# Output projection as seven half-size products, with the gate folded into sums of its weights

## The reference

```
mod = silu(c) @ ada_w + ada_b;  shift, scale, gate = split(mod, 3)
h   = rms_norm(x, norm_w) * (1 + scale) + shift
p   = h @ w_in                      # twelve kinds of columns, 4624 in all
...                                 # two mixers give o_g and o_h
m   = g_a * (o_g @ w_up_gla) + g_b * (o_h @ w_up_hgrn)
x   = x + gate * (m @ w_out)
out = rms_norm(x, final_norm_w)
```

## Time and profile before

| | us |
|---|---|
| median of 3 runs | 2876.27 |
| the profiled execution's own time | 2875.79 |
| its span, first to last instruction | 2874.0 |
| TensorE busy | 2841.4 (99%) |
| VectorE busy | 1525.2 (53%) |
| ScalarE busy | 1274.9 (44%) |
| GpSimd busy | 166.4 (6%) |
| mean granted clock of TensorE, of full speed | 0.998 |

### The profile page before, as it was taken

One profiled execution on the slowest core, in us unless ns is written; L12 is line 12 of the kernel. 1 busy time (PEld: TensorE's weight loads), 2 busy tenths in 40 slices (PEclk: granted clock), 3 DMA queues, 4 the chain that ended last, 5 costly groups with the idle time before them and its releaser, 6 DMA issues.

```text
span 2874.0 us, 38189 instructions
## 1 busy us (share of the span) xinstructions
PE 2841.4 (99%) x14534; PEld 2333.7 (81%) x14534; DVE 1525.2 (53%) x2004; ACT 1274.9 (44%) x1683; POOL 166.4 (6%) x281
## 2 busy tenths in 40 slices
PE   6999999999999999999999999999999999999998
PEld 4888888788887888888888888888888888888887
DVE  6455455644556444564555635546355463645634
ACT  3643336433473334633446433464335633355332
POOL 1010000100001000010000100001000010000100
PEclk9999999999999999999999999999999999999999
DMA  8223442233422443324432243322433224342232
GB/s 322 95 82 119 132 147 89 82 132 129 138 89 81 132 133 133 96 74 138 141 124 92 74 150 128 127 90 73 155 124 128 92 75 156 110 135 88 80 125 73
DMA packets 90205, 336.40 MB, mean 117 GB/s; under 512 B 9936, under 2 KB 10192, under 8 KB 88464
## 3 DMA queue, kind: packets, MB, share of 16 engines
q1 hardware_dynamic: 89744, 333.45, 34.9%
q10 hardware_dynamic: 256, 0.20, 0.0%
HBM read 316.63 MB, written 16.78 MB: 116 GB/s over the span
## 4 chain that ended last, share of the span: by engine, by line
PE 98%; DMA 1%; DVE 0%; ACT 0%; SPq 0%; POOL 0%; issue 0%; POOLq 0%; DVEq 0%; ACTq 0%
PE A L1041 46%; PE F L1052 33%; PE A L1103 12%; PE R L1139 1%; PE F L1166 1%; PE A L1181 1%; PE F L1160 1%; DMA ada_w<-in_ada 1%; PE R L1132 1%; PE R L1166 0%; PE R L1206 0%; PE R L1205 0%; PE R L1181 0%; PE R L988 0%; PE A L999 0%; DVE ada_w L721 0%
## 5 line engine op out<-in xcount | busy, mean ns | idle before, releaser
L676 DVE TENSOR_TENSOR w_lo<-w_raw,w_hi 128x1024 fp32r<-128x1024 f32 (+1 forms) x480 | 588.6, 1226 | 1051.0 <-ACT w_hi L453 1048.6
L453 ACT ACTIVATE w_hi<-w_raw 128x1024 fp32r<-128x1024 f32 (+1 forms) x480 | 507.3, 1057 | 753.3 <-PE A L1041 480.6
L1041 PE MATMUL A<-w_hi,h_hi 128*128 128x512 f32 (+1 forms) x1536 | 582.6, 379 | 0.0
L1041 PE MATMUL A<-w_lo,h_hi 128*128 128x512 f32 (+1 forms) x1536 | 572.9, 373 | 0.0
L1041 PE MATMUL A<-w_hi,h_lo 128*128 128x512 f32 (+1 forms) x1536 | 572.6, 373 | 0.0
L1052 PE MATMUL F<-h_hi,w_hi 128*128 128x512 f32 x1408 | 553.8, 393 | 0.0
L1052 PE MATMUL F<-h_hi,w_lo 128*128 128x512 f32 x1408 | 548.2, 389 | 0.0
L1052 PE MATMUL F<-h_lo,w_hi 128*128 128x512 f32 x1408 | 548.2, 389 | 0.0
L1041 PEld LDWEIGHTS A<-w_hi,h_hi 128*128 128x128 f32 x1536 | 288.3, 188 | 60.8 <-issue 9.0
L1041 PEld LDWEIGHTS A<-w_hi,h_lo 128*128 128x128 f32 x1536 | 288.5, 188 | 51.7
L1041 PEld LDWEIGHTS A<-w_lo,h_hi 128*128 128x128 f32 x1536 | 288.7, 188 | 47.7 <-issue 0.2
(11 more groups left out here) (180 smaller groups left out, 2790.4 us busy)
## 6 DMA issues: line engine op xcount, KB each, us to landing
w_raw<-in_w_stream SPq DMA_DIRECT2D x464, 512.0 KB, 3.5
xy<-in_x SPq DMA_DIRECT2D x8, 2048.0 KB, 8.7
result<-xy SPq DMA_DIRECT2D x32, 512.0 KB, 3.5
xf<-in_xt SPq DMA_DIRECT2D x30, 512.0 KB, 4.2
xn<-in_x SPq DMA_DIRECT2D x28, 512.0 KB, 4.9
ada_w<-in_ada SPq DMA_DIRECT2D x12, 1024.0 KB, 20.0
w_raw<-in_w_stream SPq DMA_DIRECT2D x16, 544.0 KB, 6.0
xy<-in_x SPq DMA_DIRECT2D x4, 512.0 KB, 13.9
```

Source lines behind the costliest of these rows:

```text
L453: AF(w_hi[:, s % RING, 0:n], w_raw[:, s % RAW, 0:n], ACT.Copy).then_inc(w_hi_done.sem, 1)
L676: V.tensor_tensor(w_lo[:, s % RING, 0:n], w_raw[:, s % RAW, 0:n], w_hi[:, s % RING, 0:n].bitcast(fp32), ALU.subtract).then_inc(w_split.sem, 1)
L1041: last = mm(A[t][:, 0:width], src[ia][:, k, t * P:(t + 1) * P], w_[iw][:, s % RING, kk * width:(kk + 1) * width], start=(k == 0 and n == 0 ...
```

## The change

**Seven products.** m is cut in halves of the frames (256 each) and in two halves of the features, w_out in halves of its rows and columns. Instead of eight half-size products (192 matmuls per block) there are seven, on sums and differences of the halves. A half-size product is two slots with 12 matmuls each, so the output projection has 14 slots (52 to 65) and 168 matmuls. Feature tiles are dealt to the two halves in turn (FEAT), so that pairs of tiles can be added up as they come. The pairs of banks that receive the products are `OUT_BANK`; three products are added up on top of an earlier one that VectorE has already taken (`PRODUCTS`, last field False).

**Sums of weights.** The pieces of w_out, times the gate, and their sums are made once, by GpSimd in block 0 (`out_pieces`), and written to DRAM (`pieces`, 14 of 128 by 1024). All blocks read their weights of slots 52 to 65 from there.

**Sums of m.** In every block GpSimd makes four sums of each pair of tiles (`m_sums`, four operations of 128 by 256, each waiting for the one before), ScalarE rounds them (`s_high`), and GpSimd makes the low part of three pairs (`s_low`), VectorE that of the last.

**Output.** VectorE no longer multiplies by the gate. It adds the banks into `xy` in 16 additions (`ADDS`). `xy` shares its place with the sums of m, so it is loaded later, in four parts (slots 54 and 57 of SyncE). ScalarE squares in slots 62 and 65.

**Gate later.** Parts 4 and 5 of `ada_w` are loaded behind the weights of slots 0 to 3, and worked off during slots 1 to 7 of block 0.

**Other.** `w_raw` of slots 60 to 65 uses three of its four buffers. Two of the four steps of `x_scale` and `h_low` move to slot 65. F0 uses the banks A2, A3, F0, F1.

```diff
-SLOTS = OUT0 + 8
+SLOTS = OUT0 + 14
+FEAT = [0, 4, 1, 5, 2, 6, 3, 7]
+PRODUCTS = [("m", 0, 0, 0, True), ("m", 1, 0, 1, True), ("s", 1, 1, 2, True), ("s", 0, 0, 0, False),
+            ("s", 1, 0, 2, False), ("m", 1, 1, 1, True), ("s", 0, 1, 0, False)]
+ADDS = {3: [(0, 0, 0, 0, 0), (0, 1, 1, 0, 0), (1, 0, 0, 0, 1), (1, 1, 1, 0, 2)],
+        6: [(2, 0, 2, 1, 0), (2, 1, 3, 1, 0)],
+        7: [(0, 0, 0, 1, 0), (0, 1, 1, 1, 0)],
+        9: [(2, 0, 0, 1, 7), (2, 1, 1, 1, 8)],
+        11: [(1, 0, 2, 0, 0), (1, 1, 3, 0, 0)],
+        13: [(0, 0, 2, 0, 11), (0, 0, 2, 1, 5), (0, 1, 3, 0, 12), (0, 1, 3, 1, 6)]}
-XN_AT = [49, 51, 53, 56]
+X_SCALE_AT = [49, 50, 65, 65]
+H_LOW_AT = [50, 51, 65, 65]
+RAW_AT = [s % RAW if s < 60 else (s - 60) % 3 for s in range(SLOTS)]
...
 @block.sync
             load_w(0)
-            for n in (4, 5):
-                sp.wait_ge(ada_pe, n - 3)
-                load_ada(n)
-            load_row(gate_b[:, :], 1792 + 2 * D, gate_b_in)
             for j in (2, 3):
                 load_w(j - 1)
                 load_pair(0, j, first=True)
             load_w(3)
+            sp.wait_ge(x_sq.sem, x_sq.at(0, 4))
+            load_ada(4)
+            load_row(gate_bc[:, :], 1792 + 2 * D, gate_b_in)
...
+                    if first and s == 0:
+                        sp.wait_ge(ada_pe, 4)
+                        sp.wait_ge(modT, 4)
+                        load_ada(5)
...
+                    if s in (54, 57):
+                        for t in (0, 1) if s == 54 else (2, 3):
+                            if t < 3:
+                                sp.wait_ge(s_lo_pool.sem, s_lo_pool.at(b, t + 1))
+                            else:
+                                sp.wait_ge(s_lo_dve.sem, s_lo_dve.at(b, 1))
+                            sp.dma_start(xy[:, t, :], x[bass.ds(b * T + t * P, P), :]).then_inc(xy_in[t // 2].sem, 16)
...
 @block.gpsimd
+            def out_pieces():
...
+                def gated(i, q):
+                    pool.wait_ge(b_in[i], 16 * (q + 1))
+                    two = w_b[:, i, :].rearrange("p (k n) -> p k n", k=2)
+                    cols_ = slice(512 * (i % 2), 512 * (i % 2) + 512)
+                    done(G(two, two, gate_bc[:, cols_].unsqueeze(1).broadcast_to([P, 2, 512]), ALU.mult))
+                for q in range(2):
+                    if q == 0:
+                        pool.wait_ge(ada_pe, 5)
+                    else:
+                        pool.wait_ge(pieces_out, 16 * stored[0])
+                    for i, part in ((0, 0), (2, 2), (3, 6), (1, 4)):
+                        pool.dma_start(w_b[:, i, :], w_stream[OUT0 + part + q, :, 0:1024]).then_inc(b_in[i], 16)
+                    if q == 0:
+                        pool.wait_ge(mg_used.sem, 16)
+                    for i, piece in ((0, B11), (2, B21), (3, B22)):
+                        gated(i, q)
+                        store(i, piece + q)
+                    gated(1, q)
+                    pool.wait_ge(pieces_out, 16 * stored[0])
+                    done(G(w_b[:, 0, :], w_b[:, 1, :], w_b[:, 0, :], ALU.subtract))
+                    store(0, T1 + q)
...
+            def m_sums(b, jp):
+                early, late = slice(0, T // 2), slice(T // 2, T)
+                a, c = m_raw[:, 2 * jp, :], m_raw[:, 2 * jp + 1, :]
+                pool.wait_ge(m_split.sem, m_split.at(b, 2 * jp + 2))
+                G(c[:, late], a[:, late], c[:, late], ALU.add).then_inc(m_link.sem, 1)
+                pool.wait_ge(m_link.sem, m_link.at(b, 3 * jp + 1))
+                G(a[:, late], a[:, early], a[:, late], ALU.subtract).then_inc(m_link.sem, 1)
...
+            def s_low(b, jp):
+                pool.wait_ge(s_hi_done.sem, s_hi_done.at(b, jp + 1))
+                two = slice(2 * jp, 2 * jp + 2)
+                nc.gpsimd.tensor_tensor(s_lo[:, two, :], m_raw[:, two, :], s_hi[:, two, :].bitcast(fp32),
+                                        ALU.subtract).then_inc(s_lo_pool.sem, 1)
...
+                m_sums(b, 0)
+                m_sums(b, 1)
                 if not last:
                     for t in range(NT):
                         x_tile(b + 1, t)
+                m_sums(b, 2)
+                s_low(b, 0)
+                s_low(b, 1)
+                m_sums(b, 3)
+                s_low(b, 2)
...
 @block.scalar
+            def s_high(b, jp):
+                act.wait_ge(s_sum.sem, s_sum.at(b, jp + 1))
+                two = slice(2 * jp, 2 * jp + 2)
+                AF(s_hi[:, two, :]..., m_raw[:, two, :]..., ACT.Copy).then_inc(s_hi_done.sem, 1)
...
                     if not (last and s + RING >= SLOTS):
                         split_hi(b if s + RING < SLOTS else b + 1, (s + RING) % SLOTS)
                     if s in UP_SLOT:
                         j = UP_SLOT[s]
+                        if j == KT - 1:
+                            for jp in range(3):
+                                s_high(b, jp)
                         act.wait_ge(up_used.sem, up_used.at(b, j + 1))
...
+                    if s == OUT0:
+                        s_high(b, 3)
+                    if s == OUT0 + 10:
+                        for t in (0, 1):
+                            y_square(b, t)
...
+                    if s == SLOTS - 1:
+                        for t in (2, 3):
+                            y_square(b, t)
...
 @block.vector
-                            V.tensor_tensor(y_tmp, A[t][:, :], gate_bc[:, cols_], ALU.mult).then_inc(out_used.sem, 1)
-                            dve.wait_ge(out_used.sem, out_used.at(b, 4 * n + t + 1))
-                            ins = V.tensor_tensor(xy[:, t, cols_], xy[:, t, cols_], y_tmp, ALU.add)
...
+                    if first and s in (1, 3):
+                        gate_partial(s // 2)
+                    if first and s in (5, 7):
+                        gate_column(s // 7)
...
+                    if s == OUT0 + 2:
+                        dve.wait_ge(s_hi_done.sem, s_hi_done.at(b, 4))
+                        V.tensor_tensor(s_lo[:, 6:8, :], m_raw[:, 6:8, :], s_hi[:, 6:8, :].bitcast(fp32),
+                                        ALU.subtract).then_inc(s_lo_dve.sem, 1)
+                    if s - OUT0 in ADDS:
+                        i = s - OUT0
+                        if i in (3, 6):
+                            dve.wait_ge(xy_in[i // 6].sem, xy_in[i // 6].at(b, 32))
+                        for pair_, tt, t, half, behind in ADDS[i]:
+                            if behind:
+                                dve.wait_ge(y_add.sem, y_add.at(b, behind))
+                            tile = xy[:, t, half * 512:half * 512 + 512]
+                            V.tensor_tensor(tile, tile, OUT_BANK[pair_][tt][:, :], ALU.add).then_inc(y_add.sem, 1)
...
-                    if s == 59:
-                        for t in range(NT):
+                    if s in (OUT0 + 12, OUT0 + 13):
+                        for t in (0, 1) if s == OUT0 + 12 else (2, 3):
...
 @block.tensor
-            modulation(4)
-            modulation(5)
...
+                    n, q = divmod(s - OUT0, 2)
+                    kind, f, half, pair_, fresh = PRODUCTS[n]
...
+                    if n < 2:
+                        pe.wait_ge(m_split.sem, m_split.at(b, 4 * q + 3 + n))
+                    if n == 2:
+                        if q == 0:
+                            pe.wait_ge(mg_used.sem, mg_used.at(b, 16))
+                            pe.wait_ge(s_lo_pool.sem, s_lo_pool.at(b, 2))
+                        else:
+                            pe.wait_ge(s_lo_pool.sem, s_lo_pool.at(b, 3))
+                            pe.wait_ge(s_lo_dve.sem, s_lo_dve.at(b, 1))
+                    if q == 0 and n >= 3:
+                        pe.wait_ge(y_add.sem, y_add.at(b, (2, 6, 4, 8)[n - 3]))
...
+                    if first and s in (4, 6):
+                        modulation(4 + s // 6)
```

246 lines of the change are left out of this document (144 added, 102 removed).

## The result

The changed kernel took **2919.60 us** (median of 4 runs, 2918.11 to 2922.01) against 2876.25 us for the kernel before on the same chip: a ratio of 1.0152, 95% interval 1.0134 to 1.0170. It is 43 us slower. The forecast was 2888, slower by 11.7 us, in a range from 2834 to 2903: the direction was right and the size was not, and the time lies above the range.

A forecast was written before the change was run, and what follows sets the result against it. TensorE, busy 99% of the span, was taken as the bound. Once −4.8, per block 8 × (5.3 + 0.95 − 5.44) = +6.5, boundaries +3.5 and clock +6.5 gave +11.7 us: 2888 us, range 2834 to 2903.

The forecast's parts named there:

- The earlier start: Before block 0: slot 0 starts at 41.8 instead of 51.2 us, −9.3 us.
- What block 0 gives back: Block 0: low clock at the start +1, modulation steps moved between slots +2.0, GpSimd's weight pieces holding up VectorE +1.5.
- Slot 60: The fifth product waits for VectorE's additions 5 and 6 behind the split of 61: 0.95 us late every block.
- Rivals 1 and 2: Output projection: GpSimd not held up by VectorE, 2857 us, chance 0.23; GpSimd near its lower bound, 2839 us, chance 0.20.
- the new chain at slot 56: ScalarE's s_high(3) and the split of 56 wait behind GpSimd's chain: TensorE 5.3 us late at slot 56.
- Sharing with VectorE: Slots 52 to 55: GpSimd loses 3.1 us beside VectorE's operations with two SBUF inputs, bounds 0 and 3.1.
- VectorE: m_lo of j = 7 then ends at 5.1 ... That still serves slot 55: After slot 52 starts: m_lo ends at 5.1 us instead of 3.9, still in time for slot 55, due at 8.2.
- The list of 38 us: VectorE's work in the 14 output slots: splits, additions, s_lo, x_scale, h_low and norms, 38 us in 38.1.
- Rival 3: Every block falls to the low clock and GpSimd wins over VectorE's split, making slot 55 late: 2903 us, chance 0.12.
- the block's end: Turn to the next block: the split for its slot 3 stands behind VectorE's norms, 0.5 us late seven times, 3.5 us.
- the clock: After slot 56's wait TensorE falls to the low clock in half the blocks: 4 × 1.6 = 6.5 us, bounds 0 and 21.
- SyncE's waits ... Nothing: Slots 52 to 65: SyncE's waits for s_low hold back the load of 59, which still has 4 us; no cost.

The follow-up runs named there:

- Experiment 1: Changed kernel with GpSimd's low parts of the sums of m cut to 8 of 512 columns, matmuls reading the high part instead: 2899.81 us.
- experiment 7: The kernel with all sums of m and low parts on VectorE (2860.72 us), with only the sums of m given back to GpSimd: 2869.26 us.
- experiment 6: Changed kernel with all sums of m and low parts on VectorE, h_low of the second pair at slot 55, s_high later, last squares first: 2860.72 us.
- Experiments 8 to 12: Boundary edits to the changed kernel: squares earlier (2904.87 us), loop written out (2911.21), that with two result stores behind weight loads (2899.22), stores alone (2916.98), all three (2895.68).
- experiment 8: Changed kernel with ScalarE's last two squares of a block ahead of h_high of the next block's last two pairs: 2904.87 us.
- experiment 4: Changed kernel with the three low parts that GpSimd made moved to VectorE, GpSimd keeping only the sums: 2952.36 us.
- experiment 9: Changed kernel with the loop over blocks written out on all five engines: 2911.21 us.
- experiments 13 and 14: The kernel before with only the later gate loading, with its loop (2869.98 us) and with the loop written out (2869.17 us).

## Why the prediction was right or wrong

**Right.** The removed matmuls are 5.44 us a block. The earlier start is −9.7 us (forecast −9.3). What block 0 gives back is +4.7 (forecast 1 + 2.0 + 1.5 = 4.5), but that this agrees is partly luck: the low clock at the start cost 2.4, not 1, the modulation steps 1.7, and GpSimd's pieces 0.2, not 1.5; the last 0.4 is the row of roots at slot 48. GpSimd's operations take 2.39 and 0.74 us (forecast 2.3 and 0.7). Slot 60 is 1.14 us late by the distance of the matmuls (forecast 0.95). Rivals 1 and 2 fell: GpSimd is held (1.59 us for an addition of 0.74 beside VectorE), and its operations are not near the lower bound.

**Wrong in place, and right in length by luck: the new chain at slot 56.** In the last block it stands as forecast to 0.4 us. In the seven others two things were wrong. The step named "Sharing with VectorE" let only GpSimd lose time; "no row shows VectorE being held" was true of the trace before, and I took it for nothing instead of bounding it. Held, VectorE took 3.98 us for 1.41 us of h_low, and 3.41 for a split of 1.22. And the step "VectorE: m_lo of j = 7 then ends at 5.1 ... That still serves slot 55" left h_low of the next block's second pair out of VectorE's list between m_lo and the split of 55. The list of 38 us does not show it either: it has x_scale and h_low of two pairs, as many as slot 65 alone has. Together slot 55 is 4.6 us late, slot 56 0.6, slot 60 1.1: 6.3 us, against 5.3 + 0.95 = 6.25. That the two errors moved the wait by one slot and hardly changed its length is luck; the chain itself was later than forecast, with s_high(3) 14.1 us after slot 52 in block 1 instead of 12.9.

**Rival 3 came nearest.** It had slot 55 late because GpSimd wins over VectorE, and the low clock in every block, and both came. It had a chance of 0.12 and a time of 2903, still 17 us short, since it too left the block's end at 3.5 us and gave slot 55's wait no price of its own.

The Trainium skill (SBUF — State Buffer, SBUF: two separate sides) says that of a GpSimd operation and a VectorE operation with two inputs in SBUF, whichever starts first blocks the other for its whole instruction. The trace now agrees in both directions: 0.69 to 1.48 us for m_lo and 1.22 to 3.41 for a split on VectorE, 0.74 to 1.59 for an addition on GpSimd. Experiment 1 shows what it costs by leaving out the low parts with the order unchanged, experiment 7 by giving the sums back to GpSimd; experiment 6 changed the order too.

**Mis-sized: the clock.** "I take half the blocks: 4 × 1.6" gave 6.5 us. The size of one fall was right (1.6 us at slot 55), but it came in all eight output projections, 13 us, and behind slot 3's wait in three blocks, 4.9 us. By the mean granted clock, (1 − 0.990) × 2920 − (1 − 0.998) × 2874 = 23 us of TensorE's full-speed time was lost to it, though part of this fell into waits and cost nothing. Output projection in all: forecast 8 × (6.25 − 5.44) + 6.5 = 13.0, measured 25.5. Of the 12.5 between them 6.5 are the clock, 3.2 are slot 0 of the next block, 0.4 to 0.8 late in blocks 2 to 6, and the rest is spread over slots 55 to 61.

**The step that failed most: "The block's end ... 0.5 us late, seven times, 3.5. Bounds 0 and 1.5 each".** It measured 26.0 us in all, 3.7 each. Slot 3 is 2.2 to 2.7 us late in blocks 1 to 6 and 0.5 in the last, 15.3 in sum; from slot 3 to slot 4 6.9 are lost, 4.9 of them at the lower clock and the rest mostly in waits for slot 4's weights; the row of roots takes 3.2, and 0.6 is the rest. The 3.2 us of slot 0 come on top, in the output projections' sum. The table load I named and didn't add, and the standstill of 2.5 us ahead of it can't be seen before: there the idle of the earlier trace rows is ended by TensorE. Experiments 8 to 12 show the parts: without the loop 1.9 us of slot 3's wait goes, and with it slot 0's; the stores behind the loads take slot 4's wait; and the earlier squares alone take slot 3's wait as well, since ScalarE is then through sooner. "SyncE's waits ... Nothing" looked only at slot 59: at the block's end four stores that wait for the norms stand ahead of the loads for slots 4 and 5.

The profiled execution is 34.5 us over the sum (46.2 against 11.7): 22.5 are the boundary, 12.5 the output projection, and the start with block 0 and the rest are 0.2 and 0.3 the other way.

**Left open.** Why the standstill at the loop's head is 2.5 us on ScalarE in the changed kernel and 1.3 to 1.6 in experiment 8, which changes only the order of some instructions, and grew to 6 us on VectorE in experiment 4, with no edit there. The Trainium skill (Runtime: NRT & Kernel Launch, Instruction fetch mechanics) says that a taken branch whose target is outside the two pages held forces a fetch before execution goes on. This would fit: the length differs between kernels whose code differs, it goes when the loop goes, and it is missing ahead of the last block, where no engine jumps back. No run here varied the layout alone or measured the fetch, so this cause is not shown. The share of order and of sharing in slot 55's wait is open too, beyond what experiments 1 and 7 say.

## What to carry to other kernels

Work moved to GpSimd is not free when VectorE is busy in the same stretch (34.5 of 47 us here). Take its whole duration as the upper bound of what VectorE loses, and compare that with simply doing it on VectorE (1.2 us against 2.4 here); the sums of m, moved alone in experiment 7, cost a good 1 us a block. When matmuls are taken out of a phase, every engine's list in that phase has less time, and the next wait comes where the list was already dense: check the block's boundary with all queues, that of the stores included, as closely as the edited phase. A trace cannot show what has never been late; bound a missing cost from both sides, and where no row shows one engine being held, take the row that shows the other being held.

## What was not expected of the hardware

- GpSimd holding VectorE costs up to 2.6 us on one pair of operations (3.98 against 1.41 us) and 2.2 us on one split (3.41 against 1.22).
- The head of a loop over blocks can cost ScalarE 2.5 us and a table load of 1.28 us more that the straight-line kernel does not have (7 table loads at the split's line, none in experiment 9), and VectorE 6 us (experiment 4); with nothing due there it costs less than 1 us (experiments 13 and 14: 2869.98 and 2869.17).
- After a wait of 4.4 us TensorE ran at the lower level for about 3 us (0.52 in 727 to 730), in each of the seven blocks that had it. After the waits of 2.1 to 2.6 us at slot 3 it did so in three blocks of six (0.57 in 419 to 423, 1.00 in 779 to 783).
